# Expert queries of all 256 tokens made at once, the root divided out at the scores' eviction, in a two-block transformer kernel on Trainium2

## What is computed

```python
hn2 = modulate(rmsnorm(x, norm2_g[l]), shift2, scale2)      # second block: rmsnorm alone, no shift
qh = (h @ w_q).reshape(t, PEER_HEADS, 2, PEER_HALF)         # 8 heads x 2 halves x 128
s = jnp.einsum('thcd,hcnd->thcn', qh, sub_keys)             # 128 keys each
s1, i1 = lax.top_k(s[:, :, 0], PEER_TOPK)                   # 16
s2, i2 = lax.top_k(s[:, :, 1], PEER_TOPK)
cand = s1[..., :, None] + s2[..., None, :]
top_s, pos = lax.top_k(cand.reshape(t, PEER_HEADS, -1), PEER_TOPK)
g = jax.nn.softmax(top_s, axis=-1)
pre = jnp.einsum('cd,chkd->chk', hc, u[ec])                 # 128 chosen experts per token
coef = gc * jax.nn.gelu(pre, approximate=False)
out = jnp.einsum('chk,chkd->cd', coef, v[ec])
```

## Time and profile before

| | us |
|---|---|
| median of 3 runs | 2041.39 (2035.75 to 2043.71) |
| the profiled execution | 2046.65 |
| its span, first to last instruction | 2044.8 |
| TensorE busy | 1949.5 (95%) |
| VectorE busy | 1286.7 (63%) |
| ACT busy | 501.8 (25%) |
| GpSimd busy | 359.6 (18%) |
| up-projections L1020, 2048 matmuls | 572.8 |
| down-projections L1046, 2048 matmuls | 558.0 |
| queries L993, 512 matmuls | 117.6 |

### The profile page before, as it was taken

The page is one execution under the profiler, slowest core; times in us unless marked ns, Lnnn a source line. Parts: engine busy times, 40 slices in busy tenths (PEclk is TensorE's granted clock), DMA queues, the critical chain, the costliest instruction groups (busy, mean ns, idle before and its releaser), DMA issues. The chain is left out here.

```text
span 2044.8 us, 33410 instructions
## 1 busy us (share of the span) xinstructions
PE 1949.5 (95%) x12949; PEld 1832.1 (90%) x12949; DVE 1286.7 (63%) x3204; ACT 501.8 (25%) x1734; POOL 359.6 (18%) x304
## 2 busy tenths in 40 slices
PE   4999999999999999999899889999999999999998
PEld 2887789999999999999787677789999999999998
DVE  4448423888889844444499953216897889644443
ACT  2003302213545300001214222212224444100001
POOL 0000000022332321211002720000122323222210
...
GB/s 348 398 211 96 91 144 247 267 405 378 378 401 369 403 415 413 414 413 407 134 153 108 1 92 21 124 169 299 328 411 353 398 371 401 399 414 414 413 413 217
DMA packets 123357, 604.95 MB, mean 296 GB/s; under 512 B 14588, under 2 KB 16796, under 8 KB 83136
## 3 DMA queue, kind: packets, MB, share of 16 engines
...
## 5 line engine op out<-in xcount | busy, mean ns | idle before, releaser
L1020 PE MATMUL bank<-h,ring 128*128 128x160 f32 x4096 | 572.8, 300 | 1.6 <-DMA ring<-in_ut 1.6
L1020 PEld LDWEIGHTS bank<-h,ring 128*128 128x128 f32 x4096 | 560.8, 191 | 2.1 <-DMA ring<-in_ut 2.1
L1046 PEld LDWEIGHTS bank<-expert_coef,ring 128*128 128x128 f32 x4096 | 556.9, 190 | 2.5 <-issue 1.4
L1046 PE MATMUL bank<-expert_coef,ring 128*128 128x160 f32 x4096 | 558.0, 299 | 0.7 <-DMA ring<-in_uv 0.6
L978 POOL DMA_INDIRECT expert_rows<-in_uv,pair_index x192 | 280.3, 1460 | 1299.9 <-DVEq L1412 486.3
L1262 DVE CUSTOM_DVE_ANT_0 expert_rows<-expert_rows,h_tokens 128x1024 f32<-128x1024 f32 x192 | 234.7, 1222 | 237.4 <-DMA expert_rows<-in_uv,pair_index 237.3
L1269 DVE SCALAR_TENSOR_TENSOR pair_sum<-expert_rows,pair_coef,pair_sum 128x1024 f32<-128x1024 f32 x192 | 246.0, 1281 | 56.4 <-ACT pair_coef L1165 55.1
L1163 ACT ACTIVATE pair_act<-pair_dot 128x1 f32<-128x1 f32 x192 | 38.5, 201 | 553.5 <-DVE pair_dot L1262 553.3
L993 PE MATMUL bank<-h,ring 128*128 128x128 f32 x1024 | 117.6, 278 | 6.1 <-ACT h L1172 3.8
L993 PEld LDWEIGHTS bank<-h,ring 128*128 128x128 f32 x1024 | 117.1, 194 | 7.0 <-issue 7.0
L1378 DVE TENSOR_SCALAR work<-const,choice 128x128 f32<-128x128 f32 x320 | 102.8, 343 | 0.8 <-DVE picked L1368 0.8
...
## 6 DMA issues: line engine op xcount, KB each, us to landing
ring<-in_ut SPq DMA_DIRECT2D x256, 512.0 KB
ring<-in_uv SPq DMA_DIRECT2D x256, 512.0 KB
...
```

The source lines that it names most:

```text
L1020: ins = nc.tensor.matmul(k.bank[e % 4][:, 0:DENSE], w[:, kk, :], k.h[:, kk, GATHERED:TOK], start=kk == 0, stop=kk == KD - 1)
L1046: ins = nc.tensor.matmul(down_bank(i), w[:, i * P:(i + 1) * P], A[:, e, :], start=False, stop=e == NB - 1, skip_group_check=True)
```

## The change

The first query no longer waits for the norm. With r the root of a token, W the query weights, the query is W(x * gain) / r + W(shift). The changed kernel makes W(x * gain) for all 256 tokens in one pass, from `begun`, which needs only `x` (VectorE and ACT make four of its 8 tiles each), and divides each token's scores by r when ACT copies them out of PSUM (`scale=by_token`). In the first layer two more columns of `begun` hold the shift, so a query tile has 258 columns; ACT copies the shift column out, and GpSimd adds r times it to each query tile (`tilted`). Two small matmuls turn the row of roots into a column per token (`root_columns`). The normalised tokens `k.h` are still made, for the up-projections, while the queries run.

The order on TensorE changes with it: query columns 0 to 8, the scores of columns 0 to 7 for both halves of the tokens, query columns 9 to 15, up(0), the scores of columns 8 to 15, up(1). `w_q` is loaded once per layer, and the keys stand in two places. select(0) ranks columns 0 to 7 when their scores are copied, and columns 8 to 15 when those are; select(1) is as before.

```diff
-    for name, chunks in (("in1", 10), ("v1", 4), ("ki", 1), ("in1g", 8), ("projab", 4), ("out1", 4), ("wq1", 8), ("keys1", 1), ("wq1", 8), ("keys1", 1),
+    for name, chunks in (("in1", 10), ("v1", 4), ("ki", 1), ("in1g", 8), ("projab", 4), ("out1", 4), ("wq1a", 4), ("keys1", 1), ("wq1b", 4), ("keys1", 1),
...
+        begun = flat[:, 0:KD * (TOK + SHIFT)].rearrange("p (k t) -> p k t", t=TOK + SHIFT)
+        by_dve, by_act, tilted = k.dve_emptied, k.qk_ready, k.weights_ready
+        scaled = k.sq_ready
+        normed = scaled if shift is None else k.recip_ready
...
             def _(pool):
+                if shift is not None:
+                    ch = Chain(pool, k.pool_step)
+                    shifted = tmp[:, :, :].rearrange("p a t -> p (a t)")[:, 0:TOK]
+                    for c in range(NC2):
+                        pool.wait_ge(k.act_emptied.sem, k.act_emptied.at(c + 1))
+                        if c:
+                            pool.wait_ge(tilted.sem, tilted.at(c))
+                        ch.then(nc.gpsimd.tensor_scalar(shifted, root, query_shift[:, c:c + 1], None, ALU.mult))
+                        nc.gpsimd.tensor_tensor(qt[:, c, :], qt[:, c, :], shifted, ALU.add).then_inc(tilted.sem, 1)
...
-                                               k.h[:, kk, tt * P:(tt + 1) * P], start=kk == 0, stop=kk == KD - 1)
+                            started = (by_dve, by_act)[kk % 2]
+                            pe.wait_ge(started.sem, started.at(kk // 2 + 1 + (kk % 2 and SHIFT // 2)))
+                            if kk == 0 and SHIFT:
+                                pe.wait_ge(by_act.sem, by_act.at(1))
+                        ins = nc.tensor.matmul(k.bank[c % 4][:, 0:TOK + SHIFT], w[:, kk, (c % 2) * P:(c % 2 + 1) * P],
+                                               begun[:, kk, :], start=kk == 0, stop=kk == KD - 1)
...
+                def root_columns():
+
+                    pe.wait_ge(k.rooted.sem, k.rooted.at(1))
+                    for tt in range(TT):
+                        ins = nc.tensor.matmul(k.bank[4][:, 2 * tt:2 * tt + 2], root[0:1, tt * P:(tt + 1) * P], k.ones[0:1, 0:2],
+                                               start=True, stop=True)
+                    ins.then_inc(k.turned.sem, 1)
...
+                def score(half):
+
+                    arrived(k, pe, (half + 1) * (PH // 2 + 1) - 1)
+                    keys = chunk(k, (half + 1) * (PH // 2 + 1) - 1).rearrange("p (c n) -> p c n", n=NKEYS)
+                    ready = k.act_emptied if shift is None else tilted
+                    pe.wait_ge(ready.sem, ready.at((half + 1) * HALF))
+                    if half == 0:
+                        pe.wait_ge(k.inverted.sem, k.inverted.at(1))
+                    for n in range(4 * half, 4 * half + 4):
+                        tt, low = n // 2 % 2, HALF * half + 4 * (n % 2)
+                        pe.wait_ge(k.keyed.sem, k.keyed.at(n - 3))
+                        for c in range(low, low + 4):
+                            ins = nc.tensor.matmul(k.bank[4 + n % 4][:, (c % 4) * P:(c % 4 + 1) * P],
                                                    qt[:, c, tt * P:(tt + 1) * P], keys[:, c, :], start=True, stop=True)
...
-                for tt in range(TT):
-                    for c in range(NC2):
-                        query(tt, c)
-                    score(tt)
+                query(0)
+                root_columns()
+                for c in range(1, HALF + 1):
+                    query(c)
+                score(0)
+                for c in range(HALF + 1, NC2):
+                    query(c)
...
+                    if e == 0:
+                        pe.wait_ge(normed.sem, normed.at(KD))
+                        pe.wait_ge(k.act_emptied.sem, k.act_emptied.at(NC2))
...
-                for e in range(2):
-                    up(e)
+                up(0)
+                score(1)
+                up(1)
...
+                    tt, low = n // 2 % 2, HALF * (n // 4) + 4 * (n % 2)
+                    nc.scalar.activation(s[:, tt, low:low + 4, :].rearrange("p a n -> p (a n)"),
+                                         k.bank[4 + n % 4][:, :], ACT.Copy, scale=by_token[:, tt:tt + 1]).then_inc(k.keyed.sem, 1)
+
+                def empty(c):
+                    act.wait_ge(k.tile_ready.sem, k.tile_ready.at(c + 1))
+                    if shift is not None:
+                        nc.scalar.activation(query_shift[:, c:c + 1], k.bank[c % 4][:, TOK:TOK + 1], ACT.Copy)
+                    nc.scalar.activation(qt[:, c, :], k.bank[c % 4][:, 0:TOK], ACT.Copy).then_inc(k.act_emptied.sem, 1)
+
+                def add_shift(kk):
+                    h = k.h[:, kk, 0:TOK]
+                    act.wait_ge(scaled.sem, scaled.at(kk + 1))
+                    nc.scalar.activation(h, h, ACT.Identity, bias=shift[:, kk:kk + 1]).then_inc(normed.sem, 1)
...
+                if shift is not None:
+                    nc.scalar.activation(begun[:, :, TOK:], shift.unsqueeze(2).broadcast_to([P, KD, SHIFT]), ACT.Copy)                        .then_inc(by_act.sem, 1)
+                for kk in range(1, KD, 2):
+                    nc.scalar.activation(begun[:, kk, 0:TOK], k.x[:, kk, META:], ACT.Copy, scale=gain[:, kk:kk + 1])\
+                        .then_inc(by_act.sem, 1)
+                nc.scalar.activation(root, k.bank[7][:, 0:TOK], ACT.Sqrt, bias=k.eps[:, 0:1], scale=1.0 / D)\
+                    .then_inc(k.rooted.sem, 1)
+                for c in range(HALF + 1):
+                    empty(c)
+                    if shift is not None and c >= 1:
+                        add_shift(c - 1)
+                for n in range(4):
+                    scores(n)
+                for c in range(HALF + 1, NC2):
+                    empty(c)
+                for n in range(4, 8):
+                    scores(n)
...
+                def select(tt):
+
+                    if tt == 0:
+                        dve.wait_ge(k.keyed.sem, k.keyed.at(2))
+                        rank(tt, range(HALF))
+                        dve.wait_ge(k.keyed.sem, k.keyed.at(6))
+                        rank(tt, range(HALF, NC2))
+                    else:
+                        rank(tt, range(NC2))
...
-                for tt in range(TT):
-                    half = slice(tt * P, (tt + 1) * P)
-                    ch.then(nc.vector.reciprocal(inverse[:, half], root[:, half]))
-                    for kk in range(KD):
-                        nc.vector.scalar_tensor_tensor(k.h[:, kk, half], k.x[:, kk, META + tt * P:META + (tt + 1) * P],
-                                                       gain[:, kk:kk + 1], inverse[:, half], ALU.mult, ALU.mult)\
-                            .then_inc(scaled.sem, 1)
-                dve.wait_ge(k.keyed.sem, k.keyed.at(4))
+                for kk in range(0, KD, 2):
+                    nc.vector.tensor_scalar(begun[:, kk, 0:TOK], k.x[:, kk, META:], gain[:, kk:kk + 1], None, ALU.mult)\
+                        .then_inc(by_dve.sem, 1)
+                dve.wait_ge(k.rooted.sem, k.rooted.at(1))
+                ch(nc.vector.reciprocal(inverse, root))
+                dve.wait_ge(k.turned.sem, k.turned.at(1))
+                nc.vector.reciprocal(by_token[:, :], k.bank[4][:, 0:2 * TT].rearrange("p (t n) -> p t n", n=2)[:, :, 0])\
+                    .then_inc(k.inverted.sem, 1)
+                ch.wait()
+                for kk in range(KD):
+                    nc.vector.scalar_tensor_tensor(k.h[:, kk, 0:TOK], k.x[:, kk, META:], gain[:, kk:kk + 1], inverse,
+                                                   ALU.mult, ALU.mult).then_inc(scaled.sem, 1)
                 select(0)
```

109 lines of the change are left out of this document (46 added, 63 removed).

## The result

| | before | after |
|---|---|---|
| median, us | 2039.24 (2035.75 to 2043.71, 4 runs) | 2070.97 (2066.08 to 2076.76, 4 runs) |
| ratio, 95% interval | | 1.0157 (1.0138 to 1.0176) |
| profiled execution, us | 2046.65 | 2066.08 |
| its span, us | 2044.8 | 2064.3 |

The change costs 31.7 us, 28 to 36 us by the interval. The prediction said 2072.0 us, 2060 to 2084, slower with a chance of 0.92; 30.6 us were worked out.

The account below looks back on a forecast made before the run. VectorE's chain up to TensorE's first one-hot product (L1038) was taken as the bound in both expert layers. Select(0)'s delay +32.7, gather -5.4 and clock +3.3 gave +30.6 us on 2041.39: 2072 us, range 2060 to 2084.

Parts of the forecast that it names:

- A: VectorE's chain carries select(0)'s delay to TensorE's first one-hot product in both expert layers: 2072 us, chance 0.72.
- T2: Reading from the experiments, no chance given: TensorE's stand at up(20), behind ACT's wait for the first pair, is itself the cost.
- T3: Reading from the experiments, no chance given: the loss comes from the 256-column queries or GpSimd's additions of root times shift.
- B: TensorE stays the bound and only its savings count, 4.5 us earlier in each layer: 2032 us, chance 0.04.
- C: About the same time: both gather waits and a much earlier second half of the ranking mostly absorb the delay; chance 0.04.
- D: Slower yet: GpSimd or TensorE's stand at up(20) takes over as the bound: 2085 us, chance 0.08.
- E: The shift's extra work stretches layer 1 alone: +2 to +3 us over A, 2075 us, chance 0.12.
- The delay of select(0): Its large one-hot work on VectorE starts 16.2 us later in layer 1 and 16.5 us in layer 2, together 32.7 us.
- The start: TensorE's first query in a layer begins earlier, by 2.0 us in layer 1 and 1.6 us in layer 2.
- The gather: VectorE's wait for the first gathered rows in select(1) shrinks 2.7 us per layer, -5.4 us; bounds 0 and -8.5.
- What was left in hand: VectorE has no slack at L1038, where TensorE idles 2.08 and 1.75 us, so the delay passes on undiminished.
- The clock: Low clock after TensorE's idle before L1038 costs 2.5 us per layer, +3.3 us over before; bounds -1.7 and +4.7.

Follow-up runs that it names:

- the later pairs: The changed kernel with the first pair's dot product taken up by ScalarE after up(18) instead of up(15): 2074.83 us, 1.0162 of before.
- the idle time filled: The changed kernel with columns 0-7 of tokens 128-255 ranked in VectorE's wait inside select(0): 2062.78 us; with the first pair after up(18) as well: 2068.59 us.

## Why the prediction was right, and where its working was not

**The mechanism (A) holds.** Undoing the late scores alone brought back more than the loss, and a bare delay on VectorE in the kernel before made all of it. T2 and T3 fell. B, C and D have nothing for them: the idle at the first group grew, and the stand at up(20) did not turn into the bound. E, layer 1 worse than layer 2 by the shift's work, was right in sign (13.34 against 11.68), but not in cause: without GpSimd's additions the stretch is the same, and the difference lies in layer 2 of before's trace (below).

**The delay of select(0)** was put at 16.2 and 16.5 us and measured 17.33 and 17.63. The start gave 1.82 and 1.50 us (2.0 and 1.6 predicted); the ranking halves and the small work took 390.24 - 370.35 = 19.9 us, with 19.7 in the sum. What was sized too early is the arrival of the last scores: 370.35 - 302.74 = 67.6 us into layer 1, where the sum had 375.15 - 308.46 = 66.7. Of the 0.9 us, 0.2 are the start, 0.5 lie between the first query and up(0) (the two root columns, for which no row stood, took 0.53 us and not 0.25), and 0.2 between up(0) and the copied scores.

**The gather** gave back 3.60 and 3.71 us, with 2.7 each predicted, inside the bounds of 0 and 8.5 together. The reason given for it held in the pairs of runs that differ by it alone: the changed kernel against the later pairs (0.57 and 0.62 against 4.13 and 2.73 us), and the same two with the idle time filled (1.98 and 2.13 against 6.09 and 5.88).

**What was left in hand** is the step that failed. The prediction read the 1.75 us of idle at L1038 in layer 2 as VectorE's lateness, because the row names VectorE, and so carried layer 2's delay undiminished. It was ACT's, and VectorE had 2.2 us in hand. With it the sums close: layer 1 17.33 - 3.60 = 13.7, measured 13.34; layer 2 17.63 - 3.71 - 2.2 = 11.7, measured 11.68. The bare delay closes too: 19.1 - 3.75 = 15.4 (15.0 measured), and 19.1 - 3.5 - 2.2 = 13.4 (13.4); but both are taken against the one trace of before. And there most of the 2.2 us was no lasting reserve. TensorE's waits in before (for whom, us in total, times, longest) have this row. The two waits end at 1497.81 and 1501.58 us, in layer 2's up-projections:

```profile
PE bank L1020 <- DMA ring<-in_ut: 1.6, 2, 1.3
```

They made TensorE late, not VectorE early: VectorE's share was ready 188.2 us into layer 2 and 188.5 us into layer 1. By an estimate from these rows, an execution without the two waits has 2.2 - 1.57 = 0.6 us in hand in layer 2 and loses 13.3 us there, so that the prediction's "undiminished" would be off by 0.6 us and not by 2.2. No second trace of before was taken to show it.

**The clock** was to cost 3.3 us more. In the traces it cost nothing: before had a fall behind the group of layer 1 (1.7 us lost), after has none there in spite of 3.84 us of idle, and one of 1.7 us behind the group of layer 2; other falls, with no tie to the change, balance so that the stretches behind the groups are equal to 0.14 us. Windows of 1 us behind the first group of each layer, after (busy us of TensorE, its weight loads, VectorE, ACT and GpSimd, then granted clock, DMA share, GB/s):

```profile
504.00:505.00 1.00, 0.31 (x2) 0.31 (x3) 1.00 (x5) 0.60 (x2) 0.00 (x0) 1.00 1.02 385
506.00:507.00 1.00, 1.00 (x9) 1.00 (x9) 1.00 (x2) 0.00 (x0) 0.00 (x0) 1.00 0.32 131
...
1565.00:1566.00 1.00, 1.00 (x6) 1.00 (x6) 1.00 (x4) 0.00 (x0) 0.00 (x0) 0.50 0.63 254
1566.00:1567.00 1.00, 1.00 (x6) 1.00 (x5) 1.00 (x2) 0.00 (x0) 0.00 (x0) 0.50 0.29 123
```

The Trainium skill's rule ("TensorE: Matmul & The Clock Gate", section "Why this matters for your kernels") that idle gaps bring TensorE back at half rate is borne out by 1566 us and not by 506 us. By it both layers would have paid, the 3.3 us of the prediction; this pair of traces shows none of them.

**Inside the layer.** 21.26 and 20.95 us of waiting in select(0) (21 predicted), 11.91 and 11.71 us at up(20) (11), 0.51 us at up(10) (1.4), 3.84 and 4.54 us at the first group (4 to 6), no wait ahead of the one-hot work, and the same time from the first group to the layer's end.

**The sum.** By the traces the right terms give 13.34 + 11.68 = 25.0 us, 5.6 below the sum of 30.6, which in the prediction's terms would be 2066 us and within its range; the clock (3.3) and the missed slack (2.2) are that difference, while the delay (+2.3) and the gather (-1.9) nearly cancel. The medians say 31.7, with 28 as the lower end. Against the later medians of before (2040.67 to 2042.06) the loss is 29 to 30 us. So the forecast met the medians closer than its own working deserves; that part is luck. Between the traces and the medians 4 to 7 us stay open, 1.6 of them the waits for weights that made before's traced execution longer. One trace per kernel can't show what the other executions lose, and clock falls that come in one trace and not in the next are worth 1.5 to 3 us each.
